# Attention probabilities: 1/sum applied by GpSimd ahead of the transposes, in place of a spread of 1/sum over the output

## The reference, cut to what matters

```python
def one(qblk):
    s = jnp.einsum('bqkgd,btkd->bkgqt', qblk, k, preferred_element_type=jnp.float32) * scale
    p = jax.nn.softmax(s, axis=-1).astype(v.dtype)
    return jnp.einsum('bkgqt,btkd->bqkgd', p, v)
```

## Time and profile before

| | us |
|---|---|
| median of 3 runs (3627.19 to 3630.64) | 3627.91 |
| the profiled execution, its own time | 3628.72 |
| its span, first to last instruction | 3626.9 |

### The profile page before, as it was taken

How to read it: one execution, slowest core, us unless ns; L and a number is a source line. 1 busy time by engine, 2 the same in 40 slices (tenths; PEclk the granted TensorE clock), 3 DMA queues, 4 the chain that set the end, 5 groups by cost and what they waited for, 6 DMA issues and landing times.

```text
span 3626.9 us, 51892 instructions
## 1 busy us (share of the span) xinstructions
PE 3240.7 (89%) x16852; PEld 2549.8 (70%) x16856; DVE 1797.8 (50%) x3260; ACT 1115.3 (31%) x1951; POOL 1090.8 (30%) x683
## 2 busy tenths in 40 slices
PE   6788699999989788999979888999999678899997
PEld 3656588888867566998946546788778445578876
DVE  4666777753355764432436465434231367743324
ACT  3144241111131564322222123432231045543222
POOL 1121122323223212444423210444444112234443
PEclk8789899999999898999989796999999669999999
DMA  6101234433111002233212100233323100023332
GB/s 236 58 0 59 93 110 139 145 127 99 55 44 46 1 2 69 83 97 93 87 58 64 43 1 4 87 96 95 93 87 93 47 1 1 1 76 95 96 93 81
DMA packets 74331, 258.60 MB, mean 71 GB/s; under 512 B 9456, under 2 KB 12016, under 8 KB 72688
## 3 DMA queue, kind: packets, MB, share of 16 engines
q1 hardware_dynamic: 60256, 205.61, 18.5%
q10 hardware_dynamic: 13968, 51.65, 4.3%
HBM read 253.03 MB, written 2.10 MB: 70 GB/s over the span
## 4 chain that ended last, share of the span: by engine, by line
PE 79%; DVE 7%; issue 6%; ACT 4%; DVEq 1%; ACTq 1%; POOL 1%; DMA 1%; SPq 0%; POOLq 0%; PEldq 0%
PE ps L773 54%; PE ps L751 6%; PE ps L1964 3%; PE ps L1978 3%; PE ps L1162 2%; PE ps L416 1%; PE ps L1167 1%; DVE ps L379 1%; PE ps L2126 1%; PE ps L919 1%; PE ps L2158 1%; ACT w_hi L612 1%; PE ps L2120 1%; DVE rot_s L955 1%; DVE nm L1204 1%
## 5 line engine op out<-in xcount | busy, mean ns | idle before, releaser
L719 POOL TENSOR_TENSOR w_lo<-w_raw,w_hi 128x1024 fp32r<-128x1024 f32 (+1 forms) x373 | 917.9, 2464 | 1791.0 <-ACT w_hi L612 1790.9
L612 ACT ACTIVATE w_hi<-w_raw 128x1024 fp32r<-128x1024 f32 (+1 forms) x373 | 385.7, 1039 | 1289.9 <-PE ps L773 1054.6
L773 PE MATMUL ps<-h_hi,w_hi 128*128 128x258 f32 (+2 forms) x1824 | 321.7, 330 | 52.8 <-ACT w_hi L612 48.5
L773 PEld LDWEIGHTS ps<-h_hi,w_hi 128*128 128x128 f32 x1824 | 272.9, 195 | 87.3 <-issue 39.4
L773 PE MATMUL ps<-h_lo,w_hi 128*128 128x258 f32 (+2 forms) x1824 | 309.0, 322 | 0.0
L773 PE MATMUL ps<-h_hi,w_lo 128*128 128x258 f32 (+2 forms) x1824 | 307.6, 321 | 0.0
L773 PEld LDWEIGHTS ps<-h_lo,w_hi 128*128 128x128 f32 x1824 | 265.7, 191 | 27.0
L773 PEld LDWEIGHTS ps<-h_hi,w_lo 128*128 128x128 f32 x1824 | 264.8, 190 | 27.5
L1964 PE MATMUL ps<-keys,qs 128*128 128x256 f32 (+3 forms) x672 | 178.2, 376 | 59.8 <-POOL qs L1130 53.3
L1204 DVE TENSOR_REDUCE nm<-ps 128x1 f32<-128x512 f32 (+5 forms) x304 | 178.0, 586 | 94.3 <-PE ps L1966 45.8
L1261 ACT ACTIVATE probs<-ps,nm 128x512 f32<-128x512 f32 (+5 forms) x304 | 184.3, 606 | 111.7 <-DVE nm L1204 45.4
(11 more groups left out here) (304 smaller groups left out, 5256.9 us busy)
## 6 DMA issues: line engine op xcount, KB each, us to landing
w_raw<-in_ffn_in SPq DMA_DIRECT2D x176, 512.0 KB, 3.6
mod_row<-in_w_mod_rows ACTq DMA_DIRECT2D x80, 512.0 KB, 4.4
w_raw<-in_ffn_out SPq DMA_DIRECT2D x64, 512.0 KB, 3.6
w_raw<-in_ev_in SPq DMA_DIRECT2D x26, 512.0 KB, 3.6
w_raw<-in_ffn_out SPq DMA_DIRECT2D x32, 384.0 KB, 3.0
w_raw<-in_od_in SPq DMA_DIRECT2D x21, 512.0 KB, 3.6
mod_ring<-in_w_mod SPq DMA_DIRECT2D x8, 1024.0 KB, 13.1
w_raw<-in_wo_in SPq DMA_DIRECT2D x12, 512.0 KB, 3.6
```

Of the source, the lines that this page charges most:

```text
L612: act.activation(k.w_hi[:, s, 0:self.KT * P], k.w_raw[:, s, 0:self.KT * P], ACT.Copy).then_inc(k.sems["w_hi_ready"], 1)
L719: ins = pool.tensor_tensor(k.w_lo[:, s, 0:self.KT * P], k.w_raw[:, s, 0:self.KT * P], k.w_hi[:, s, 0:self.KT * P].bitcast(F32), ALU.subtract)
L773: ins = pe.matmul(k.ps[:, 2 * s + g, 0:t1 - t0], w[:, s, c * P:(c + 1) * P], h[:, c, t0:t1], start=(n == 0), stop=(n == len(parts) - 1))
```

## The change

GpSimd multiplies each unit's probabilities, in place, by 1/sum (repeated over the columns) before TensorE transposes them. It waits for VectorE's reciprocal (semaphore `rinv_ready`), and TensorE's transposes wait for it (`prepared`). The four spread matmuls of a batch, ScalarE's copy and VectorE's multiply by it go; VectorE copies the output from PSUM at the batch's end, or adds it where results are added. The casts that stage the next turn's queries stand behind the batch's four multiplies in GpSimd's order, wait for these (`prepared`), and GpSimd waits for its casts (`q_staged`) before it goes on.

```diff
@@ gpsimd
-        if not self.queries:
+        if not self.scaled:
             return
+        def normal(j, u):
+            a, qi, *_ = self.units[u]
+            p = k.probs[:, u % 2, 0:len(self.tiles(qi)) * P]
+            pool.wait_ge(k.sems["rinv_ready"], self.g(j, u, "rinv_ready", 1))
+            pool.tensor_tensor(p, p, k.rinv[:, u:u + 1].to_broadcast([P, len(self.tiles(qi)) * P]), ALU.mult).then_inc(k.sems["prepared"], 1)
...
         for n in range(self.B):
             move(0, n)
+        pool.wait_ge(k.sems["q_staged"], self.b_q + 4 * self.B)
 
         def turn(j, last):
             for n in range(self.B):
-                u = self.Z * (n + 1)
+                for u in range(self.Z * n, self.Z * (n + 1)):
+                    normal(j, u)
                 if not last:
+                    u = self.Z * (n + 1)
+                    pool.wait_ge(k.sems["prepared"], self.g(j, u, "prepared"))
 
                     pool.wait_ge(k.sems["scores_ready"], self.g(j, u, "scores_ready"))
                     move(j + 1, n)
+                    pool.wait_ge(k.sems["q_staged"], j * (4 * self.B) + (self.b_q + 4 * (self.B + n + 1)))
@@ vector
-            chain_ins.then_inc(S["prepared"], 1)
+            chain_ins.then_inc(S["rinv_ready" if self.scaled else "prepared"], 1)
...
-                done = "spread_ready" if self.spread else "pv_ready"
-                dve.wait_ge(S[done], self.gb(j, n, done, 1))
+                dve.wait_ge(S["pv_ready"], self.gb(j, n, "pv_ready", 1))
@@ scalar
-            if i == self.Z - 1 and self.spread:
-                act.wait_ge(S["pv_ready"], self.gb(j, n, "pv_ready", 1))
-
-                act.wait_ge(S["o_free"], self.gb(j, n, "o_free"))
-                act.activation(k.spread[:], k.ps[:, 6 + n % 2, 256:512], ACT.Copy).then_inc(S["spread_ready"], 1)
+            pass
@@ pair_pv
-            made = [lambda i=i, a=a: pe.matmul(o[64 * a:64 * a + 64, 256 + i * P:256 + (i + 1) * P],
-                                               k.rinv[:, units(n, a, i):units(n, a, i) + 1].to_broadcast([P, HD]), k.ident[:],
-                                               start=True, stop=True, skip_group_check=True)
-                    for i in range(2) for a in range(2)]
-            return made + [lambda i=i, a=a, slot=slot, t=t, c0=c0, c1=c1: pe.matmul(
+            return [lambda i=i, a=a, slot=slot, t=t, c0=c0, c1=c1: pe.matmul(
@@ finish
-            return dve.tensor_tensor(dst(j, n), o[:, 0:256].unsqueeze(1), k.spread[:].unsqueeze(1), ALU.mult)
+            return dve.tensor_copy(dst(j, n), o[:, 0:256].unsqueeze(1))
@@ the causal stages' finish
-                chain.link(dve.tensor_tensor(k.part[:], o[:, 0:256], k.spread[:], ALU.mult))
-                return dve.tensor_tensor(dst, dst, k.part[:].unsqueeze(1), ALU.add)
+                return dve.tensor_tensor(dst, dst, o[:, 0:256].unsqueeze(1), ALU.add)
```

More of the change, by code:

```diff
@@ L1028, with __init__ @@
 class Attend(Stage):
-    def __init__(self, kit, J, batches, scores, tiles, slots, pv, prepare, marks, finish, pt, spread=False, sink=None, unroll=False, queries=None):
+    def __init__(self, kit, J, batches, scores, tiles, slots, pv, prepare, marks, finish, pt, scaled=False, sink=None, unroll=False, queries=None):
         super().__init__(kit)
@@ L1219, in prepare @@
                 chain.link(chain_ins)
-                dve.wait_ge(S["prepared"], self.g(j, u, "prepared"))
+                if not self.scaled:
+                    dve.wait_ge(S["prepared"], self.g(j, u, "prepared"))
                 chain_ins = self.prepare(dve, chain, j, u, a, qi, k.probs[:, u % 2, 0:len(self.tiles(qi)) * P], k.rinv[:, u:u + 1])
-            chain_ins.then_inc(S["prepared"], 1)
+            chain_ins.then_inc(S["rinv_ready" if self.scaled else "prepared"], 1)
         def unit(j, u, there):
@@ L1809, in memory @@
     k.keys4 = [at(f"keys4{n}", [P, 2, 2, SEQ], F32R, o) for n, o in enumerate((H + 34816, W + 8192, W + 16384))]
-    k.spread = at("spread", [P, 256], F32, H + 47104)
-    k.part = at("part", [P, 256], F32, H + 48128)
     k.rot_c = at("rot_c", [P, 2, SEQ], F32, W + 8192)
@@ L2018, in plan @@
            lambda qi: list(range(6)), lambda n, qi: 0,
-           pair_pv(lambda a, t: k.v_tok0[:, t, a * HD:(a + 1) * HD], lambda n: [(t, t, 0, 256) for t in range(6)], k.pt6, unit4),
-           None, no_marks, times_spread(lambda j, n: o0[:, ds(j), 256 * n:256 * n + 256]), k.pt6, spread=True,
+           pair_pv(lambda a, t: k.v_tok0[:, t, a * HD:(a + 1) * HD], lambda n: [(t, t, 0, 256) for t in range(6)], k.pt6),
+           None, no_marks, put(lambda j, n: o0[:, ds(j), 256 * n:256 * n + 256]), k.pt6, scaled=True,
            queries=queries(k.qkv_hi, k.lo_0, 0, 0))
@@ L2214, in gated, with add_out @@
                 return dve.tensor_tensor(rinv, rinv, k.gates[:, qi, dsx(j, 3, (8 * grp + 4 * a) * 3 + gate, 1)], ALU.mult)
[L2216 removed]
+            def add_out(dve, chain, o, j, n, grp=grp):
                 dst = k.o_t[:, ds(j, 4 * grp), 256 * n:256 * n + 256]
[L2218 to L2219 removed]
+                return dve.tensor_tensor(dst, dst, o[:, 0:256].unsqueeze(1), ALU.add)
             def scores(pe, s, j, a, qi, grp=grp, keys=k.keys4[(2 * kind + grp) % 3]):
@@ L2227, in plan @@
             Attend(k, 4, [four(0), four(1)], scores, causal_tiles, lambda n, qi: 0,
-                   pair_pv(lambda a, t, grp=grp, v_tok=v_tok: v_tok[:, t, (2 * grp + a) * HD:(2 * grp + a + 1) * HD], causal_terms, k.pt4, unit4),
-                   gated, (lambda u: 0, 1), add_spread, k.pt4, spread=True, queries=queries(k.qkv2_hi, k.lo_3, 4 * grp, 4 * grp))
+                   pair_pv(lambda a, t, grp=grp, v_tok=v_tok: v_tok[:, t, (2 * grp + a) * HD:(2 * grp + a + 1) * HD], causal_terms, k.pt4),
+                   gated, (lambda u: 0, 0), add_out, k.pt4, scaled=True, queries=queries(k.qkv2_hi, k.lo_3, 4 * grp, 4 * grp))
     Split(k, [(k.o_t[:, m, :], *in_ha(m)) for m in range(8)], chunks=range(8))
```

18 lines of the change are left out of this document (8 added, 10 removed).

## The result

The changed kernel takes **3696.95 us** (median of 4 runs, 3694.13 to 3701.33), the kernel before 3627.55 beside it: a ratio of 1.0197, 95% interval 1.0174 to 1.022. It is slower by 2%. The forecast was 3694, range 3650 to 3745. The profiled execution took 3699.69 us, its span 3697.5.

What follows compares the result with a forecast made beforehand. The prediction took TensorE, nearly full in the first stage, as the bound, with GpSimd's multiply lengthening the loops after the change. Its terms, 18 + 3 + 29 + 16 = 66 us, on 3628.7 gave 3694 us, range 3650 to 3745.

Steps and rivals of the forecast that it cites:

- Added: 240 GpSimd multiplies: GpSimd, attention stages: multiplies priced on a two-input line, 0.13 us plus 2.2 ns a column, 1.83 us for 768.
- First stage: First layer's attention: multiply, scores and maximum in the loop, 11.8 us a batch against 9.86; +18 us.
- Context part: First layer's context units: multiplies of 0.70 us, short loop through 1/sum, some 0.2 us for 16 units; +3 us.
- Window stages: Two window stages: the first stage's loop with 640 columns, 10.5 us a batch against 8.68; +29 us.
- Causal stages: Four causal stages: multiplies, casts and gate handoffs on GpSimd, +1.0 us a turn over 16 turns; +16 us.
- GpSimd's own queue fills: Causal stages: multiplies 6.7 us, casts 3.6, handoffs 2.4 and 0.6 make 13.3 us a turn against 12.5.
- the sum 16 us lower: Causal stages: without the port lock the gate runs beside the multiply, the turn is hidden, and the +16 us goes.
- Moved and waited for: GpSimd's casts now behind four multiplies: costed at nothing in first and window stages; 1 us a batch if slack is gone.
- The granted clock falls: Rival: TensorE, partly idle, is granted a lower clock in wide and part of causal batches; +45, about 3740 us; chance 0.17.
- The multiply is hidden: Rival, first and window stages: 768 columns stay under 0.55 us, up to 35 us come back, 3593; chance 0.06.
- One-input price: Rival: multiplies cost 1.2 ns a column, 0.92 us for 768, so no change, about 3625 us; chance 0.06.
- halfway to the high bound: Rival: contention with VectorE makes each wide multiply in the loop 0.45 us longer; 19 + 27, or 3740 us; chance 0.12.

Runs made afterwards that it cites:

- E1: Changed kernel with GpSimd multiplying only the first 128 columns of each unit (output not the reference's): 3626.3 us, ratio 1.0000 to the kernel before.
- E6: Changed kernel with VectorE taking 1/sum of unit u+1 before the maximum of unit u+2: 3736.6 us, ratio 1.0299 to the kernel before.
- E10: Changed kernel with casts copying only 16 of 256 query columns from each stage's second turn (output not the reference's): 3658.8 us, ratio 1.0092.
- E9: Changed kernel with the changes of E2 and E6 together: 3718.8 us, ratio 1.0283 to the kernel before.
- E2: Changed kernel with VectorE's three small two-input operations rewritten with a column as scalar: 3703.3 us, ratio 1.0210 to the kernel before.
- E11: Changed kernel, but VectorE builds a rounded diagonal of 1/sum and TensorE scales while transposing, in one pass: 3639.0 us, ratio 1.0045.
- E8: Changed kernel with the multiply by 1/sum and gate on VectorE, GpSimd only staging queries: 3631.2 us, ratio 1.0016 to the kernel before.

## Why the prediction was right, and where its steps were not

The sum was +66; the eight stages lost 66.6. That is luck: the steps miss by up to 13.5 us, in both directions. With the multiplies as long as they turned out, the prediction's own sums give 12 us for the first stage, 3 for the context part and 20.5 for the windows, and for a causal turn 12.3 us against 12.5, which is nothing: about 36 in all, or 3664. A multiply priced some 30 us too dear stood in for a causal loss of 29.5 us whose cause the prediction did not have.

- **Added: 240 GpSimd multiplies**, mis-sized. I took 1.83 us for 768 columns from the two-input rows; it was 1.47, 1.68 ns a column, about halfway between my one-input and my two-input line. The second operand is not free, but a repeated column costs less than a full one.
- **First stage**, +18 forecast, +10.8 measured. With 1.47 in place of 1.83 the forecast's own loop is 5.56 us, 11.1 a batch; measured 11.14 and 11.47. The loop is the right mechanism: E1 (its length) and E6 (VectorE's order) each shorten the stage, by 14.2 and 7.8 us.
- **Context part**, +3 forecast, +2.2 measured.
- **Window stages**, +29 forecast, +24.1 measured: the same multiply too long (0.53 us a batch, 8 us), and against it the casts, costed at nothing, of which E10 took away less than half and 10.8 us came back. By these two the sum would be 31 or more, so I also read the loop itself at least 7 us too long. E9 against E2 points to the step: taking the scores and the maximum out of the way of 1/sum is worth only 4.7 us in both windows, so they held the loop less there than in the first stage, whose reading I had carried over.
- **Causal stages**, +16 forecast, +29.5 measured: the largest miss. A batch is 7.54 us (GpSimd's casts start at 3136.41, 3143.87, 3151.39 and 3159.03), not 6.8. GpSimd's items do stand in the chain: shorter multiplies alone (E1) take back 27.7 us, shorter casts alone (E10) 25.2. But "GpSimd's own queue fills" is wrong: GpSimd is busy 57% of these stages (143.6 of 252.5 us) and waits between. Wrong too is the step that was to fill it, a handoff of 0.3 us for every gate behind a multiply, and with it "the sum 16 us lower" without the lock: in E2 there is no lock and the stages are 3.4 us longer. What I had left out is the round trip through two probability buffers, as these rows of the changed kernel have it:

```profile
3153.31 1.77 POOL L1130 TENSOR_TENSOR probs<-probs,rinv 128x384 f32<-128x384 f32 x2 [0.16 <-POOL qs L1137]
...
3154.27 0.43 PE L1174 MATMUL ps<-ident,probs 128*128 128x128 f32 x2 [0.36 <-POOL probs L1130]
...
3155.02 0.68 ACT L1273 ACTIVATE probs<-ps,nm 128x512 f32<-128x512 f32 x1
...
3155.45 0.69 DVE L1216 TENSOR_REDUCE nm<-ps 128x1 f32<-128x512 f32 x1
...
3156.06 0.15 DVE L1229 RECIPROCAL rinv<-rowsum 128x1 f32<-128x1 f32 x1
...
3156.61 2.17 POOL L1130 TENSOR_TENSOR probs<-probs,rinv 128x512 f32<-128x512 f32 x2 [1.52 <-DVE rinv L2215]
```

  From one pair of multiplies GpSimd waits 1.52 us for transposes, copy, exponential and 1/sum of the unit that takes over the buffer, before the next pair. VectorE is at a maximum (to 3156.14) when the row sum is there, so the maximum does hold 1/sum here, by some 0.2 us, which the prediction had ruled out for these stages. The chain goes round, multiply and casts both in it, so GpSimd is at once waited for and waiting. That the two buffers close it is read from the rows, with E1 and E10 behind it; a kernel with a third buffer, which would test it directly, was not run.
- **Moved and waited for**: "I cost it at nothing" failed. The slack of 2 us a batch was in GpSimd's total, not at the place of the casts; there 1/sum was ready while they ran.
- **The granted clock falls**, the rival at 0.17: not in the wide stages (1.00 in the first stage from 227 us on; 0.92 and 0.94 in the windows against 0.92 and 0.96), where TensorE stayed busy for 84% of the first stage and not for the two thirds that I gave it, but in the causal ones, 0.82 to 0.88 against 0.90 to 0.97. TensorE's 1089 records there are busy for 193.5 us in the changed kernel and 178.4 in E1, which has the same records. How much of these 15 us lies on the chain is not separated.
- **The multiply is hidden**, the rival that decides at 0.55 us: E1 has 0.40 us and its wide stages are indeed below before, but by 6 us where I had allowed for up to 35.
- **One-input price** is excluded by the 1.47 us; **halfway to the high bound** by the same row.

## What to carry to other kernels

An engine that is nearly empty is a place for work only if the work is off the loop: here GpSimd took 1.47 us between 1/sum and the transposes, with two buffers, and the stage grew by 10.8 us while TensorE's own work in it did not. Before moving an operation, write the loop down with the buffers that close it, place every other item of the receiving engine's queue on it (casts that were free behind a wait were not free behind a multiply), and ask what the same operation costs on the engine that already stands there: VectorE did it in 0.63 us, and in the stages where it could also take in the gate that was a gain. If stages differ, choose per stage.

## What the runs showed of the hardware that I had not expected

- **Nearly a whole stage at the lower clock with TensorE full.** The first causal stage of E11 (stretch, its length, TensorE busy with its records, granted clock; us):

```profile
2950.00:2963.00 13.00, 0.00 (x0) 0.50 0.00 0
2963.00:2973.00 10.00, 8.07 (x32) 0.50 0.00 0
2973.00:2990.00 17.00, 17.00 (x69) 0.50 0.00 1
2990.00:3010.00 20.00, 19.34 (x96) 0.67 0.00 1
3010.00:3030.00 20.00, 19.42 (x78) 0.50 0.00 0
```

  The kernel before, the same stretch:

```profile
2950.00:2963.00 13.00, 0.00 (x0) 0.50 0.00 0
2963.00:2973.00 10.00, 7.75 (x42) 0.66 0.01 3
2973.00:2990.00 17.00, 15.82 (x120) 1.00 0.01 1
```

  Both come out of an idle stretch at 0.50, which is 1.2 GHz. The one is at 2.4 GHz from 2973 us on, the other stays at the lower level for most of 60 us more, and its stage takes 68.2 us where E11's other three take 51.3, 53.3 and 52.4. Why is open, but it is no accident of one execution: the mean granted clock of E11's nine runs is 0.906 to 0.915 (the profiled one 0.914), that of the kernel before in the twelve runs beside them 0.921 to 0.929. E11's context part was granted 0.65 as well, against 0.88, and took 39.7 us where the kernel before takes 34.7. As far as nine runs show, the lower clock comes with this kernel, and its total of 3639.0 holds what it costs.
- **A lock is worth what stands on it.** The same rewriting of three small operations changed the windows by +2.8 us in one order (E2 against the changed kernel) and by -14.6 in another (E9 against E6).
- **VectorE's multiply slows GpSimd.** In E8 a pair of casts that takes 0.85 us alone takes 1.16 beside it:

```profile
248.76 1.16 POOL L1130 CAST qs<-lo 64x256 fp32r x2
...
249.04 0.62 DVE L1223 TENSOR_SCALAR probs<-probs,rinv 128x768 f32<-128x768 f32 x1
```

  The Trainium skill (SBUF - State Buffer, "SBUF: two separate sides") lets a VectorE operation in a mode with two ports take the same lock; the longer cast agrees with it. The multiply itself began 0.28 us into the casts and took 0.62 us, about the mean of all of its width (0.632), so these rows do not show it held up in turn.
